# Forming the low parts of the weights on POOL instead of DVE inside the attentions of a two-layer hybrid diffusion backbone

## What is computed

```
def token_mixers(u, uc, w_in, ...):
    t = mixer_inputs(jnp.split(u @ w_in, IN_OFFSETS, axis=-1), ropes, *mla_w)
    s = mixer_inputs(jnp.split(uc @ w_in, IN_OFFSETS, axis=-1), None, *mla_w)
    y_a, y_a_c = window_gqa(t['a_q'], ..., a_sink, with_ctx)
    y_b, y_b_c = mlstm_bidir(t['b_q'], ..., b_gate_bias, with_ctx)
    y_c, y_c_c = mla_attn(t['c_qn'], ..., with_ctx)
    y_d, y_d_c = diff_attn(t['d_q'], ..., lam, lam_init, d_g_sub, with_ctx)
    y = merge_branches((y_a, y_b, y_c, y_d), t['gates'], w_branch, w_out)
    ...

def joint_softmax(scores, sink=None):
    m = scores[0].max(axis=-1, keepdims=True)
    ...
    e = [jnp.exp(s - m) for s in scores]
    den = sum(ei.sum(axis=-1, keepdims=True) for ei in e)
    ...
    return [ei / den for ei in e]

def merge_branches(ys, gate_logits, w_branch, w_out):
    g = jax.nn.sigmoid(gate_logits.reshape(gate_logits.shape[:2] + (N_BRANCH, D_MODEL)))
    merged = sum(g[:, :, i] * (y @ w_branch[i]) for i, y in enumerate(ys))
    return merged @ w_out
```

## Time and profile before

| | us |
|---|---|
| median of 3 runs | 3787.38 (3786.98 to 3789.18) |
| the profiled execution | 3781.9 |
| its span, first to last instruction | 3780.2 |
| PE busy | 3286.8 (87% of the span) |
| DVE busy | 1802.1 (48%) |
| ACT busy | 1004.6 (27%) |
| POOL busy | 408.8 (11%) |

### The profile page before, as it was taken

One profiled execution on the slowest core, in us unless ns is written; L12 is line 12 of the kernel. 1 busy time (PEld: TensorE's weight loads), 2 busy tenths in 40 slices (PEclk: granted clock), 3 DMA queues, 4 the chain that ended last, 5 costly groups with the idle time before them and its releaser, 6 DMA issues. The chain is left out here.

```text
span 3780.2 us, 45802 instructions
## 1 busy us (share of the span) xinstructions
PE 3286.8 (87%) x17846; PEld 2934.8 (78%) x17846; DVE 1802.1 (48%) x3302; ACT 1004.6 (27%) x1522; POOL 408.8 (11%) x276
## 2 busy tenths in 40 slices
PE   6977999988999888699999968699879998879997
PEld 5966997887789678599999958577767796658785
DVE  6666135423337674576111375724433376543334
ACT  2211224413221433211211222123423324332221
POOL 0001000010011001222022020100010010111011
PEclk6987999998999999799999979799989999889998
DMA  5500220121124003152221232032121250233332
GB/s 182 162 14 12 56 90 24 62 78 40 34 103 138 23 23 130 73 154 84 72 61 53 82 122 92 1 78 78 38 92 51 67 173 23 77 124 89 94 90 94
DMA packets 328783, 295.82 MB, mean 78 GB/s; under 512 B 39502, under 2 KB 307996, under 8 KB 326812
## 3 DMA queue, kind: packets, MB, share of 16 engines
q1 hardware_dynamic: 315406, 229.74, 20.4%
q10 hardware_dynamic: 13198, 63.65, 4.5%
HBM read 262.54 MB, written 30.41 MB: 77 GB/s over the span
## 5 line engine op out<-in xcount | busy, mean ns | idle before, releaser
L720 PE MATMUL ps<-u_hi,w_hi 128*128 128x384 f32 (+1 forms) x2592 | 759.8, 354 | 69.4 <-ACTq L391 19.1
L720 PE MATMUL ps<-u_lo,w_hi 128*128 128x384 f32 (+1 forms) x2592 | 752.3, 351 | 0.0
L720 PE MATMUL ps<-u_hi,w_lo 128*128 128x384 f32 (+1 forms) x2592 | 751.8, 351 | 0.0
L1407 DVE TENSOR_TENSOR w_lo<-w_raw,w_hi 128x2048 fp32r<-128x2048 f32 x155 | 378.3, 2441 | 582.5 <-ACT w_hi L1080 581.3
L720 PEld LDWEIGHTS ps<-u_hi,w_hi 128*128 128x128 f32 x2592 | 477.0, 191 | 107.3 <-issue 46.1
L720 PEld LDWEIGHTS ps<-u_lo,w_hi 128*128 128x128 f32 x2592 | 479.7, 190 | 25.4
L720 PEld LDWEIGHTS ps<-u_hi,w_lo 128*128 128x128 f32 x2592 | 478.3, 190 | 26.0
L1080 ACT ACTIVATE w_hi<-w_raw 128x2048 fp32r<-128x2048 f32 x155 | 296.4, 1913 | 537.0 <-PE ps L720 297.5
L1108 ACT ACTIVATE space<-ps 128x768 f32<-128x768 f32 (+3 forms) x158 | 117.4, 745 | 702.5 <-PE ps L720 691.0
L882 PE MATMUL ps<-space 128*128 128x128 f32 (+1 forms) x1472 | 209.8, 290 | 72.6 <-DVE space L1680 63.3
L882 PEld LDWEIGHTS ps<-space 128*128 128x128 f32 x1472 | 184.4, 199 | 109.8 <-DVE space L1680 82.5
(11 more groups left out here) (227 smaller groups left out, 4480.0 us busy)
## 6 DMA issues: line engine op xcount, KB each, us to landing
w_raw<-in_w_in SPq DMA_DIRECT2D x288, 256.0 KB, 4.1
space<-in_w_mod SPq DMA_DIRECT2D x48, 1024.0 KB, 5.4
w_raw<-in_w_gate_up SPq DMA_DIRECT2D x176, 256.0 KB, 4.0
w_raw<-in_w_down SPq DMA_DIRECT2D x96, 192.0 KB, 2.8
w_raw<-in_w_branch SPq DMA_DIRECT2D x64, 256.0 KB, 3.6
h_scratch<-space ACTq DMA_DIRECT2D x4, 3072.0 KB, 9.3
space<-h_scratch ACTq DMA_DIRECT2D x4, 3072.0 KB, 10.0
m_scratch<-space ACTq DMA_DIRECT2D x3, 3072.0 KB, 10.8
```

Source lines behind the costliest of these rows:

```text
L720: last = nc.tensor.matmul(ps[:, 2 * (t % 2) + b, 0:a1 - a0], wv[w][:, k, j * P:(j + 1) * P], xx[:, k, a0:a1], start=(k == 0 and w == 0 and ...
L1407: V.tensor_tensor(w_lo[slot][:, :], w_raw[slot][:, :], w_hi[slot][:, :].bitcast(F32), ALU.subtract).then_inc(w_lo_done, 1)
```

## The change

Within the attentions the pieces on DVE are gone. POOL waits for the high part of the unit (`w_hi_done`) and forms the whole low part in one operation of 2048 columns (L2075 in the changed kernel), four for each attention, 24 in all. In d the inverse roots (L2040 in the changed kernel, `d_root`) are placed between these operations: after the low part of unit v come `queries * (v + 1) // 4 - queries * v // 4` roots.

```
--- before.py
+++ after.py
@@ -1599,23 +1599,6 @@
-                span = jobs_a_unit(l, kind)
-                parts = 2 if span == 4 else 4
-
-                def fill_split(i):
-
-                    v, at = i // span, i % span - 2
-                    u = g.u0 + v + 1
-                    slot = u % 2
-                    if at == 0:
-                        dve.wait_ge(w_hi_done, u + 1)
-                    if 0 <= at < parts:
-                        part = slice(at * (UNIT // parts), (at + 1) * (UNIT // parts))
-                        last = V.tensor_tensor(w_lo[slot][:, part], w_raw[slot][:, part],
-                                               w_hi[slot][:, part].bitcast(F32), ALU.subtract)
-                    if at == parts - 1:
-                        last.then_inc(w_lo_done, 1)
-
@@ -1734,7 +1717,6 @@
                 for i in range(len(jobs)):
-                    fill_split(i)
                     if kind == "d":
...
+            def d_root():
+                n.rms += 1
+                pool.wait_ge(rms_in, n.rms)
+                G.tensor_tensor(rms_d[:, 0, :], rms_d[:, 1, :], half_neg[:, 0:1].to_broadcast([P, HEADS]),
+                                ALU.pow).then_inc(rstd_d, 1)
...
-                elif kind == "attend" and arg[0] == "d":
-                    for _ in range(len(attend_jobs(l, arg[0])) // HEADS):
-                        n.rms += 1
-                        pool.wait_ge(rms_in, n.rms)
-                        G.tensor_tensor(rms_d[:, 0, :], rms_d[:, 1, :], half_neg[:, 0:1].to_broadcast([P, HEADS]),
-                                        ALU.pow).then_inc(rstd_d, 1)
+                elif kind == "attend":
+                    queries = len(attend_jobs(l, arg[0])) // HEADS if arg[0] == "d" else 0
+                    for v in range(arg[1].n):
+                        u = arg[1].u0 + v + 1
+                        pool.wait_ge(w_hi_done, u + 1)
+                        G.tensor_tensor(w_lo[u % 2][:, :], w_raw[u % 2][:, :], w_hi[u % 2][:, :].bitcast(F32),
+                                        ALU.subtract).then_inc(w_lo_done, 1)
+                        for _ in range(queries * (v + 1) // arg[1].n - queries * v // arg[1].n):
+                            d_root()
```

## The result

| | before | after |
|---|---|---|
| median, us | 3787.5 (4 runs, 3787.0 to 3789.2) | **3836.2** (4 runs, 3829.3 to 3837.9) |
| the profiled execution, us | 3781.9 | 3837.8 |
| its span, us | 3780.2 | 3836.1 |

The ratio of the changed kernel to the one before is 1.0127, 95% interval 1.0112 to 1.0143: 48.6 us slower. That lies in the predicted range, 34.8 us under the predicted 3871, and 6 us from the 3842 of the rival "one-element operations pass".

The account below looks back on a forecast made before the run. PE was taken as nearly full, DVE's pieces mostly hidden. Waits of 28 (a), 3 (c), 17.6 and 12.5 (d), less 2, make 59 us; with 25 us of clock, 84 us on 3787.4 gives 3871 us, range 3824 to 3900.

Parts of the forecast that it names:

- one-element operations pass: Rival: DVE's one-element operations are not held; a loses 22 us, c nothing, d 17.6; 3842 us with clock; chance 0.26.
- What bounds the kernel: Attentions: PE is nearly full; DVE's pieces stand in time spent waiting for PE, except around normalisations in d.
- The 2 us in d0: Pieces leaving DVE in four jobs of d0 with a normalisation gain some 0.5 us each, 2 us in all.
- The cost of the low part: On POOL: each of 24 subtractions of 2048 columns takes 4.5 us, extrapolated from 512 and 768 columns.
- The lock: Between POOL and DVE: a blocked DVE operation cannot start until POOL's whole operation of 2048 columns is over.
- Which operations are blocked: On DVE: those with two SBUF inputs and small SBUF-to-SBUF ones, L1642, L1645 and L1660 included; PSUM readers pass.
- a, waits: Windowed attention, eight units: DVE's L1642 stands still until POOL ends and PE waits behind it, together 28 us.
- d, behind a root: Differential attention, four units: POOL goes from root to low part, L1723 waits about 4.4 us each, 17.6 us.
- d, L1645: Differential attention, the four other units: L1645 is held and PE's next scores come later, 12.5 us together.
- clock: Behind new or lengthened PE waits in a, c and d: 17 lower-clock stretches of 1.5 us, 25 us.
- Twice as slow: Rival: POOL's own low part stretches to 9 us beside DVE in all 24 units; 3980 us; chance 0.04.
- nothing blocked: Rival: PE has unseen slack or blocks fall on DVE's idle time, only the 2 us stay; 3785 us; chance 0.06.

Follow-up runs that it names:

- experiments 2, 4 and 11: 2: kernel before, POOL's low part in c alone, 1.0001; 4: changed kernel, addition as tensor_scalar, 3801.5 us; 11: kernel before, POOL in a and c, that addition, 3783.9 us.
- experiment 8: Kernel before with each DVE piece cut to 8 columns, the rest of the low parts not formed: 3783.3 us, 0.9991 of before.
- Experiment 9: Changed kernel with POOL's low part cut into four operations of 512 columns back to back: 3797.4 us, 1.0025 of before.
- experiment 5: Kernel before with the addition of the sink's share in a as a tensor_scalar, as a control: 3786.2 us, 1.0000 of before.
- experiment 6: Changed kernel in which POOL in d also waits until DVE's running normalisation is over: 3833.9 us, 1.0126 of before.

## Why the prediction was right or wrong

**What bounds the kernel: right.** DVE's pieces were hidden in a and c; taking them away brings nothing there (experiments 2, 4 and 11). The 2 us in d0 fit experiment 8, which can't tell them from nothing.

**The cost of the low part: right.** 4.5 us each, worked out from rows 4. It is exactly six steps of 0.54 us from 512 to 2048 columns, not six and a bit. Only two of the 24 took longer, 4.9 us at most, where DVE's mixing was already running.

**The lock: right in kind, and for the whole of an operation.** The rows had POOL operations of 1.8 us and less; the 4.5 us ones hold DVE back to their end, as the Trainium skill says in "SBUF — State Buffer", section "SBUF: two separate sides": 4.48 us in the changed kernel. Experiment 9 adds that between two operations the other engine gets in.

**Which operations are blocked: wrong, and this is the step that failed.** From L1813, with four elements, I went to L1642, L1645 and L1660, with one. L1813's reading was sound and did not reach that far. The runs showed 0.14 us for one element and 4.42 us for two at the same moment, and none of 240 one-element tensor_scalar operations held. The Trainium skill, in "VectorE: DVE Perf Modes", section "What auto-detection actually checks", gives a single-source operation between SBUF tiles the mode that uses both ports where the outermost non-unit dimensions are both even or equal. Two elements meet that, and the trace agrees with 4.42 us. A lone element has no non-unit dimension, so that sentence says nothing for the forecast and against the rival; the measurement decides. What hung on this step:

| term | predicted | rival | measured |
|---|---|---|---|
| a, waits | 28 | 22 | 22.4 (PE idle) |
| c | 3 | 0 | 0 |
| d, behind a root | 17.6 | 17.6 | 4 x 4.3 = 17.2 (L1706) |
| d, L1645 | 12.5 | 0 | 0 |
| pieces | -2 | -2 | some -2.6 in d0 (one hold of 4.3, PE idle 1.7 more), not told from 0 (experiment 8) |
| waits, sum | 59 | 37 | 37.3 (PE idle, six attentions) |
| clock | 25 | 18 | 14.7 (PE busy) |

The last two rows hold for the sum of the six attentions, 52 us; the four entries above them are not independent measurements of it (22.4 + 17.2 with the predicted -2 is 37.6, where the idle time is 37.3). The whole span grew by 55.9 us; the other 4 us lie outside the attentions, and as much moves between executions of kernels that are alike: the control of experiment 5 has a span of 3786.6 us, 6.4 over the one of before, with the same median.

**The clock: a fifth too large even for the rival, 18 for 14.7 us.** In a there are eight new waits and 13.6 us more of busy PE, 1.7 us each, near my 1.5. The error was the extra stretch that I gave to each wait made longer. In d1 three waits went from some 4 to 8 us, and PE's busy time grew by 0.4 us. Behind the wait of 8.32 us the view by stretch shows

```profile
3219.30:3223.30 4.00, 3.94 (x19) 3.86 (x20) 3.72 (x9) 1.41 (x3) 0.00 (x0) 0.59 0.76 256
```

that is 4 x (1 - 0.59) = 1.6 us lost, as much as the 1.5 us behind the shorter wait. Here a wait paid its slow stretch once, behind its end, at 4 us as at 8.

**The number and the luck.** The measured 3836 us lie in the range only because the range was drawn down to the rival's 3824. By the forecast's own sum of waits with no clock loss at all, 3787.4 + 59 = 3846 us, the time could not have come so low. Its 12.5 us in d and 3 us in c did not exist. In a its 40 us for the measured 36 rest on the wrong operation: in the unit of rows 8 the hold is 2.4 us, on L1653, where the forecast had 3.65 on L1625. The rival had the mechanism, and its 3842 us are 6 us off.

**Slips in the sum that change nothing.** 4.3 - 1.4 is 2.9 and not 3.0; and 16 pieces with 9.6 us are 0.25% of the time, so the bound of 0.2% is reached at 13.

**The other rivals.** "Twice as slow" (3980) falls with POOL's 4.5 us, "nothing blocked" (3785) and "faster" with the eight and four long operations.

**Signs given ahead.** Right: POOL's 4.5 to 4.9 us, the normalisation's tail over 4 us three times in d1, PE's longest wait over 8 us, c1 unchanged, and the sign that tells the rival apart (L1653 long, L1625 never). Wrong: the few long executions of L1625, and growth of d0 and d1 by 18 and 22 us, measured 2 and 13. a0 and a1 came near, 17 and 19 against 20 and 20.

The chance was misplaced too. In the trace of the kernel before no one-element operation of DVE starts inside one of POOL's, so it could not decide between the two; what I had was one operation with four elements, and I gave 0.62 to it against 0.26. What that trace could have shown is that "from SBUF to SBUF" is no sufficient sign of being held. This shuffle from SBUF to SBUF stands inside POOL's rotary product and keeps its time:

```profile
531.13 1.30 POOL L1991 TENSOR_TENSOR space<-space 128x512 f32<-128x512 f32 x1 [11.19 <-DVEq L1593]
...
531.19 0.75 DVE L1584 STREAM_SHUFFLE space<-space 128x512 f32<-128x512 f32 x1
```

## What to carry to other kernels

An operation on the neighbouring engine costs what it holds back, not what it takes: list, for the whole length of POOL's operation, each DVE operation with two tensor sources in SBUF and each tensor_scalar from SBUF to SBUF with more than one element a partition, and ask who stands behind it. Where one tiny operation is the first in that list, its form can be changed (33 us of 48.6 here), and POOL's operation can be cut so that DVE gets in between; but moving it past one blocked operation only pays if the next one isn't of the same kind. Work taken from a hidden place on DVE brought nothing here (c alone: 1.0001 of before).

## What the runs showed of the hardware that was not expected

- Beside a running POOL operation a DVE tensor_scalar of one element a partition passes (0.14 us, also with a one-element scalar from SBUF: 0.20, and with two: 0.27), and one of two elements waits for POOL's end (4.42 us). A tensor_tensor of one element waits too (4.48 us). Reciprocals pass, with one element and with two (L1641, 0.15 us at 3208.82 in experiment 6, inside POOL's operation), and so does a shuffle of 512 columns from SBUF to SBUF (L1584 in the kernel before, 32 executions, 17 of them started inside an operation of POOL's, none over 0.77 us). What of the chip makes this difference wasn't tried further; the number of elements alone is not it, as these two show.
- POOL's operations back to back let DVE in between: single waits of at most 1.25 us in a in place of 4.48, and POOL's third operation then takes 1.7 us, longer by what DVE had still to run.
- A PE wait that grows from 4 to 8 us brings no second stretch at the lower clock: 1.6 us lost behind it, 1.5 before.
